# Retention's query times state in two parts, and a split last half of the attention's output

## The reference

```python
def step(r, qkv):                     # retention, chunk by chunk, per head
    s = einsum('bihd,bjhd->bhij', qf, kf) * intra
    o = einsum('bhij,bjhe->bihe', s, vf)
    o = o + einsum('bihd,bhde->bihe', qf, r) * q_dec
    r = r * c_dec + einsum('bjhd,bjhe->bhde', kf * k_dec, vf)
# then head_norm(o) * silu(g), a product with w_out, and a gate
# second layer: o = softmax(q k^T + decays) v, per head; x + gate * ((o * silu(g)) @ w_out)
```

## Time and profile before

| | us |
|---|---|
| median of 3 runs | 1717.95 (1715.57 to 1719.02) |
| the profiled execution's own time | 1717.91 |
| its span in the profile | 1716.1 |
| PE busy | 1661.4 (97%) |
| DVE busy | 812.5 (47%) |
| ACT busy | 611.4 (36%) |
| POOL busy | 380.7 (22%) |

### The profile page before, as it was taken

The page is one execution under the profiler, slowest core; times in us unless marked ns, Lnnn a source line. Parts: engine busy times, 40 slices in busy tenths (PEclk is TensorE's granted clock), DMA queues, the critical chain, the costliest instruction groups (busy, mean ns, idle before and its releaser), DMA issues.

```text
span 1716.1 us, 22075 instructions
## 1 busy us (share of the span) xinstructions
PE 1661.4 (97%) x8377; PEld 1326.9 (77%) x8377; DVE 812.5 (47%) x1661; ACT 611.4 (36%) x999; POOL 380.7 (22%) x501
## 2 busy tenths in 40 slices
PE   4999999999999999999999999999999998999998
PEld 3999998777876766667668888888788886788887
DVE  4654442212245445545543333665654015777774
ACT  4311121111134434434440223623322116566663
POOL 2111112111233333333322223414211100111000
PEclk8999999999999999999999999999999999999999
DMA  9544545563456767577663312232223625555531
GB/s 314 198 154 164 181 145 204 178 215 134 164 166 202 245 190 235 178 225 240 200 237 119 111 38 85 101 103 69 94 89 98 204 99 154 182 177 166 170 134 59
DMA packets 145338, 275.40 MB, mean 160 GB/s; under 512 B 18099, under 2 KB 64335, under 8 KB 145234
## 3 DMA queue, kind: packets, MB, share of 16 engines
q1 hardware_dynamic: 112450, 181.92, 33.2%
q0 software_dynamic: 32784, 92.08, 15.7%
HBM read 193.51 MB, written 80.43 MB: 160 GB/s over the span
## 4 chain that ended last, share of the span: by engine, by line
PE 84%; DVE 6%; ACT 4%; issue 3%; DMA 2%; POOL 1%; SPq 0%; DVEq 0%; POOLq 0%; ACTq 0%
PE trunk_ps L1150 29%; PE in_ps_o L541 12%; PE in_ps_o L537 11%; PE trunk_ps L1145 5%; PE tail_ps L2117 5%; PE tail_ps L2108 3%; PE trunk_ps L1193 3%; PE trunk_ps L1177 3%; PE tail_ps L2068 2%; PE tail_ps L2081 2%; PE in_ps_o L562 1%; PE trunk_ps L1188 1%; DVE room L1590 1%; POOL room L1460 1%; PE trunk_ps L1253 1%
## 5 line engine op out<-in xcount | busy, mean ns | idle before, releaser
L1150 PE MATMUL trunk_ps<-w_hi,hT_hi 128*128 128x512 f32 x880 | 360.0, 409 | 0.6 <-DVE w_lo L210 0.6
L1150 PE MATMUL trunk_ps<-w_hi,hT_lo 128*128 128x512 f32 x880 | 349.4, 397 | 0.0
L1150 PE MATMUL trunk_ps<-w_lo,hT_hi 128*128 128x512 f32 x880 | 347.0, 394 | 0.0
L1150 PEld LDWEIGHTS trunk_ps<-w_hi,hT_hi 128*128 128x128 f32 x880 | 165.5, 188 | 54.9 <-issue 17.6
L1150 PEld LDWEIGHTS trunk_ps<-w_lo,hT_hi 128*128 128x128 f32 x880 | 165.4, 188 | 43.0 <-issue 5.0
L1150 PEld LDWEIGHTS trunk_ps<-w_hi,hT_lo 128*128 128x128 f32 x880 | 165.2, 188 | 39.2
L210 DVE TENSOR_TENSOR w_lo<-w_raw,w_hi 128x1024 fp32r<-128x1024 f32 x76 | 96.5, 1271 | 115.3 <-ACT w_hi L198 110.0
L537 PE MATMUL in_ps_o<-hT_hi,w_hi 128*128 128x384 f32 x384 | 130.5, 340 | 0.4 <-DVE hT_lo L675 0.4
L537 PE MATMUL in_ps_o<-hT_hi,w_lo 128*128 128x384 f32 x384 | 129.1, 336 | 0.0
L537 PE MATMUL in_ps_o<-hT_lo,w_hi 128*128 128x384 f32 x384 | 129.1, 336 | 0.0
L541 PE MATMUL in_ps_o<-w_hi,hT_hi 128*128 128x512 f32 x288 | 114.4, 397 | 0.0
(11 more groups left out here) (274 smaller groups left out, 3291.8 us busy)
## 6 DMA issues: line engine op xcount, KB each, us to landing
w_raw<-in_a_w_in SPq DMA_DIRECT2D x96, 256.0 KB, 3.4
room<-in_state_ret SPq DMA_DIRECT2D x64, 256.0 KB, 4.0
out_state_sample<-room POOLq DMA_DIRECT2D x64, 256.0 KB, 6.7
room<-in_b_ada_w SPq DMA_DIRECT2D x24, 512.0 KB, 6.9
scratch_qkT<-room POOLq DMA_DIRECT2D x48, 192.0 KB, 2.2
scratch_v_hi<-room POOLq DMA_DIRECT2D x36, 256.0 KB, 2.6
scratch_v_lo<-room POOLq DMA_DIRECT2D x36, 256.0 KB, 3.1
scratch_o<-room POOLq DMA_DIRECT2D x36, 256.0 KB, 3.3
```

Source lines behind the costliest of these rows:

```text
L1150: ins = pe.matmul(ps[:, bank, :], h[:, k, t * P:(t + 1) * P], w[:, (C0 + j) % 2, k, :], start=k + m == 0, stop=k == KT - 1 and m == 2)
```

## The change

In the retention:

- the query chunk times state is done in six fp32r products (L1183 after the change) instead of two in float32 (L1193). For them ACT copies the new state (128x1024) and the next query chunk (128x256) into fp32r tiles (`hi_made`), and DVE subtracts (`query_low`, L1618, and `state_low`, L1623), for chunks 1 to 7 of each head;
- to make room, the values have one buffer in place of two: `load_v` of the next chunk waits for the output of this one (`o_done`), and stands in POOL's program ahead of this tile's gate product;
- queries and keys come chunk by chunk, 36 loads of 256 KB in pieces of 512 bytes, into three slots, where there were portions of three chunks; a slot is free once its chunk is scored and its query is split;
- `split_lo` moves from the end of an odd tile to the next even tile, behind `new_strips`, `query_low` and `state_low` and ahead of `statistics`; the fourth quarter so stands in tile 8;
- the rows that `half_turn` reads use other semaphores, with the same waits.

In the attention: in the last query tile, one output product each moves from units 4 and 6 to unit 7, where both stand behind the last turn of weights and ahead of the last values; the DVE's evacuation moves with them. The second half of the last tile is split in two quarters of 256 columns, in two banks, each with its own evacuation, addition and store.

```diff
-        v_hi, v_lo = (part(o, 2 * DV).rearrange("p (a b) -> p a b", a=2) for o in (0, 2 * DV))
-        k_hi, k_lo = part(4 * DV, DK), part(4 * DV + DK, DK)
-        s_hi, s_lo = part(4 * DV + 2 * DK, P), part(4 * DV + 2 * DK + P, P)
+        v_hi, v_lo = part(0, DV), part(DV, DV)
+        k_hi, k_lo = part(2 * DV, DK), part(2 * DV + DK, DK)
+        s_hi, s_lo = part(2 * DV + 2 * DK, P), part(2 * DV + 2 * DK + P, P)
+        state_hi, state_lo = pr.state_hi, pr.state_lo
+        q_hi, q_lo = pr.q_parts[:, 0], pr.q_parts[:, 1]
...
-        qk = [at(9216, 4, NB3), at(11776, 4, NB3)]
+        qk = [at(9216 + 4 * P * i, 4, P) for i in range(3)]
...
+        def qk_landed(h, c):
+            g = score_no(h, c)
+            return qk_in[g % 3], 16 * (g // 3 + 1)
 
...
+                h, c = g // T, order[g % T]
+                if g >= 3:
+                    ph, pc = (g - 3) // T, order[(g - 3) % T]
+                    sp.wait_ge(scored, g - 2)
+                    if pc == SELF:
                         sp.wait_ge(qs_ready, ph + 1)
+                    elif pc:
+                        sp.wait_ge(q_split, 7 * ph + pc)
                 for sem_, per_head in pr.qk_stored:
...
+                src = dr["qkT"][4 * h:4 * h + 4, :, c * P:(c + 1) * P].rearrange("a p t -> p a t")
+                sp.dma_start(qk[g % 3], src).then_inc(qk_in[g % 3], 16)
...
+                    if h + t == 0:
+                        load_qk(3)
+                    if T * h + t + 4 < T * RH:
+                        load_qk(T * h + t + 4)
...
-                    pe.wait_ge(state_new, n)
-                    q, _ = qk_of(h, c)
+                    pe.wait_ge(q_split, 7 * h + c)
+                    pe.wait_ge(state_split, 7 * h + c)
                     for a in range(2):
-                        ins = pe.matmul(ps[:, PS_O, :], q[:, a, :], state[:, a, :], start=False, stop=a == 1)
+                        for m, (q, r_) in enumerate(((q_hi, state_hi), (q_hi, state_lo), (q_lo, state_hi))):
+                            ins = pe.matmul(ps[:, PS_O, :], q[:, a, :], r_[:, a, :], start=False, stop=a == 1 and m == 2)
...
+                    if t + 1 < PT:
+                        act.wait_ge(state_new, PT * h + t + 1)
+                        act.copy(state_hi[:, :, :], state[:, :, :]).then_inc(hi_made, 1)
+                        act.wait_ge(*qk_landed(h, t + 1))
+                        act.copy(q_hi, qk_of(h, t + 1)[0]).then_inc(hi_made, 1)
...
-                if n >= 2:
-                    ph, pc = divmod(n - 2, PT)
+                if n:
+                    ph, pc = divmod(n - 1, PT)
                     pool.wait_ge(o_done, ph * T + pc + 1)
                 for dst, src in ((v_hi, "v_hi"), (v_lo, "v_lo")):
-                    pool.dma_start(dst[:, n % 2], dr[src][c * P:(c + 1) * P, h * DV:(h + 1) * DV].bitcast(F32R)).then_inc(v_in[n % 2], 16)
+                    pool.dma_start(dst, dr[src][c * P:(c + 1) * P, h * DV:(h + 1) * DV].bitcast(F32R)).then_inc(v_in, 16)
 
...
+                    if t < PT and PT * h + t + 1 < RH * PT:
+                        load_v(PT * h + t + 1)
...
+            def query_low(h, c):
+
+                dve.wait_ge(hi_made, 14 * h + 2 * c)
+                dve.tensor_tensor(q_lo, qk_of(h, c)[0], q_hi.bitcast(F32), ALU.subtract).then_inc(q_split, 1)
+
+            def state_low(h, c):
+
+                dve.wait_ge(hi_made, 14 * h + 2 * c + 1)
+                dve.tensor_tensor(state_lo[:, :, :], state[:, :, :], state_hi[:, :, :].bitcast(F32), ALU.subtract).then_inc(state_split, 1)
...
+                    if 0 < t < PT:
+                        query_low(h, t)
+                        state_low(h, t - 1)
                     if h == RH - 1:
                         half_low(t, 0)
+                    if t and t % 2 == 0:
+                        split_lo(pr, dve, C0 + h + 1, (C0 + h + 1) % 2, t // 2 - 1, gain=pr.gn_g[:, 0] if h + 1 == NG else None)
...
-                    if t % 2 and t < 2 * SUBS:
-                        split_lo(pr, dve, C0 + h + 1, (C0 + h + 1) % 2, t // 2, gain=pr.gn_g[:, 0] if h + 1 == NG else None)
...
-    COUNT = [[0, 2, 3, 3, 3, 2, 3, 0], [3, 2, 2, 1, 3, 2, 3, 0], [3, 1, 4, 0, 4, 0, 4, 0]]
+    COUNT = [[0, 2, 3, 3, 3, 2, 3, 0], [3, 2, 2, 1, 3, 2, 3, 0], [3, 1, 4, 0, 4, 0, 4, 0], [3, 1, 4, 0, 3, 0, 3, 2]]
+    HALF = CW // 2
...
+            def last_half(part, heads):
+
+                cols = slice(part * HALF, (part + 1) * HALF)
+                for h in heads:
+                    for m, (a, w) in enumerate(((oT_hi[:, h, :], pr.w_hi), (oT_hi[:, h, :], pr.w_lo), (oT_lo[:, h, :], pr.w_hi))):
+                        ins = pe.matmul(ps[:, part, 0:HALF], a, w[:, 1, h, cols], start=h + m == 0, stop=h == FH - 1 and m == 2)
+                if FH - 1 in heads:
+                    ins.then_inc(end_done, 1)
...
-                    count = COUNT[0 if s == 1 else 1 + order[s] // 4]
+                    count = COUNT[0 if s == 1 else 1 + (order[s] + 1) // 4 - int(order[s] == 3)]
...
-            for h in range(4):
-                end(STEPS - 1, 1, h, 0)
+            pe.wait_ge(o_split, 2 * (STEPS - 1) + 1)
+            for part in range(2):
+                last_half(part, range(4))
...
-                if s and i == 6:
+                if s and i == (7 if s + 1 == STEPS else 6):
...
+            last = 2 * (STEPS - 1)
+            for n, (c0, c1, bank) in enumerate(((0, CW, END), (CW, CW + HALF, 0), (CW + HALF, D, 1))):
+                width, into = c1 - c0, c0 % CW
+                dve.wait_ge(end_done, last + n + 1)
+                dve.wait_ge(added, last + n)
+                dve.tensor_tensor(tmp[:, into:into + width], ps[:, bank, 0:width], gate[:, c0:c1], ALU.mult).then_inc(end_out, 1)
+                if n < 2:
+                    dve.wait_ge(x1_in[n], 16 * STEPS)
+                dve.wait_ge(end_out, last + n + 1)
+                dve.tensor_tensor(x1[:, c0:c1], x1[:, c0:c1], tmp[:, into:into + width], ALU.add).then_inc(added, 1)
```

More of the change, by code:

```diff
@@ L823, in trunk @@
         ps_t = ps[:, 4:8, :].rearrange("p (a b) c -> p a b c", a=2)
-        qk_in = [sem(f"qk_in{i}") for i in range(2)]
-        v_in = [sem(f"v_in{i}") for i in range(2)]
+        qk_in = [sem(f"qk_in{i}") for i in range(3)]
+        v_in, hi_made, q_split, state_split = sem("v_in"), sem("hi_made"), sem("q_split"), sem("state_split")
         parted = sem("parted")
@@ L1050, in _ @@
                 sp.wait_ge(sem_, count)
-            load_qk(0)
+            for g in range(3):
+                load_qk(g)
             sp.dma_start(cols[:, :, :], pr.table["cols"].rearrange("p (a b) -> p a b", a=RH)).then_inc(cols_in, 16)
@@ L1058, in _ @@
             load_weights(1, 1)
-            load_qk(1)
             load_r(1)
@@ L1510, in _ @@
                     pool.dma_start(dr["o"][t * P:(t + 1) * P, h * DV:(h + 1) * DV], o_t).then_inc(o_stored[n % 2], 16)
-                    if t < PT and 8 * h + t + 2 < RH * PT:
-                        load_v(8 * h + t + 2)
             for n in range(M0, N):
@@ L2001, in _ @@
                 load_residual(STEPS - 1, c)
-            for c in range(2):
-                sp.wait_ge(added, 2 * STEPS - 1 + c)
-                sp.dma_start(rows_of(STEPS - 1, c)[0], x1[:, c * CW:(c + 1) * CW]).then_inc(y_last, 16)
-            sp.wait_ge(y_last, 32)
+            last = rows_of(STEPS - 1, 0)[0], *(rows_of(STEPS - 1, 1)[0][:, part * HALF:(part + 1) * HALF] for part in range(2))
+            for n, (c0, c1) in enumerate(((0, CW), (CW, CW + HALF), (CW + HALF, D))):
+                sp.wait_ge(added, 2 * STEPS - 1 + n)
+                sp.dma_start(last[n], x1[:, c0:c1]).then_inc(y_last, 16)
+            sp.wait_ge(y_last, 48)
         @block.tensor
@@ L2150, in _ @@
                 end(STEPS - 1, 0, h, END)
-            for h in range(4, FH):
-                end(STEPS - 1, 1, h, 0)
+            for part in range(2):
+                last_half(part, range(4, FH))
         @block.scalar
@@ L2407, in _ @@
             low_part(STEPS, 1)
-            for c in range(2):
-                end_out_of(STEPS - 1, c, 0 if c else END)
-                half = x1[:, c * CW:(c + 1) * CW]
-                dve.wait_ge(x1_in[c], 16 * STEPS)
-                dve.wait_ge(end_out, 2 * (STEPS - 1) + c + 1)
-                dve.tensor_tensor(half, half, tmp, ALU.add).then_inc(added, 1)
+            last = 2 * (STEPS - 1)
[8 more added lines that the diff above has]
+                dve.tensor_tensor(x1[:, c0:c1], x1[:, c0:c1], tmp[:, into:into + width], ALU.add).then_inc(added, 1)
 def build(nc, dram, table):
```

72 lines of the change are left out of this document (23 added, 49 removed).

## The result

The changed kernel takes **1733.37 us** (median of 4 runs, 1729.11 to 1735.37), the kernel before 1717.43 (4 runs); the ratio is 1.0088, with a 95% interval of 1.0076 to 1.0100. It is slower by some 15 us where 5 less were forecast, and outside the range. The profiled execution took 1732.21 us, its span is 1730.4.

What follows compares the result with a forecast made beforehand. PE, busy in 97% of the span, was taken as the bound; gains of 9.2, 7.0, 1.0 and 2.7 less costs of 5.8 and 8.8 made 5.3, so 1717.9 would become 1712.6 us, range 1703 to 1724.

Steps and rivals of the forecast that it cites:

- Query times state: Retention: six fp32r matmuls instead of two float32 ones save PE 0.33 us in each of 28 outputs, minus 9.2 us.
- Low weights behind the strips: Retention, tiles 4 and 6: PE's 0.88 us wait for the strips' banks goes, 8 times, minus 7.0 us.
- Tile 8: Retention: the fourth quarter of low weights comes late, PE waits 1.75 us in three heads, 0.5 in the last; plus 5.8.
- Values in one buffer: Retention, tiles 3, 5 and 7: values land late by 0.5 twice and 1.2 once in each head, plus 8.8 us.
- SP's queue: Retention, odd tiles: the query chunk's load stands behind a waiting weight load; no cost, as PE already waits for values.
- The last head's rows: Retention, tile 1 of the last head: the 1.8 us wait for half_turn's rows shrinks as PE comes later, minus 1.0.
- rival 3: Retention, tile 8: after each of four waits PE runs at the lower clock, 1.7 us each, 1719.4 us; chance 0.12.
- The attention's end: Attention's last query tile: moved products fill a gap and keep the clock up, 1.7 of the total; minus 2.7 us.
- Rival 2: Retention, odd tiles: values, query chunk and weights crowd; loads are the bound, 2 us late gives 1727.8 us; chance 0.18.

Runs made afterwards that it cites:

- split_alone: Kernel before with query times state in two parts in heads 0 to 2, two value pairs, chunk load ahead of weights, tile 1 reordered: 1717.35 us.
- one_pair: Kernel before with its values in one buffer, asked for when an output is done and ahead of the gate product: 1728.56 us, ratio 1.0057.
- qk_first: Changed kernel with the next query chunk's load ahead of the weight loads on SP's queue: 1725.36 us, ratio 1.0049.
- low_behind: Kernel before with the first three quarters of low weights behind the strips of tiles 2, 4 and 6: 1710.77 us, ratio 0.9957.
- tail_alone: Kernel before with only the change's part at the attention's end: 1715.81 us, ratio 0.9991.
- quarter_4: Changed kernel with the fourth quarter of low weights back at the end of tile 7: 1730.18 us, ratio 1.0076.

## Why the prediction was wrong

**Query times state, minus 9.2: right.** In tile 4 the first of the six starts at 639.10 and the next product at 640.46, 1.36 us against 1.72; 28 times 0.36 is 10.1. The low state is waited for once (0.5). From the start of the update to that of the product's second matmul it is 3.75 (636.94 to 640.69) against 4.10 in tile 5 before (641.85 to 645.95), 0.35 less. But split_alone shows that without the next term it is worth nothing; I had summed the two as independent.

**Low weights behind the strips, minus 7.0: right**, 7.2 by itself; in the changed kernel too no wait for the strips' banks is left before tile 8 of the last head.

**Tile 8, plus 5.8: right.** Three waits of 1.44 and one of 0.65, each 0.25 longer than listed, are 6.0:

```profile
581.25 0.50 PE L1141 MATMUL trunk_ps<-w_hi,hT_hi 128*128 128x512 f32 x1 [1.44 <-DVE w_lo L210]
```

**Values in one buffer, plus 8.8: right in size, partly by luck.** Eight waits of 7.2, 9.2 with the uncounted part, and some 10 in one_pair. But I had twelve, in tiles 3, 5 and 7 of every head; two of the eight stand in tile 1, none in the last head, and in three odd tiles the chunk's wait came first. By the Trainium skill ("DMA: Bandwidth & Descriptors", "Bandwidth") the loads would have landed later than my median. The time did come out slower, but not in that way: the value loads landed sooner than before (median 4.5 in heads 0 to 2, against 6.2), only they were asked for later.

**SP's queue, "I cost them at nothing of their own": this step failed.** The times that I gave the chunk were right: it goes out about when the values do (614.59 and 615.29) and is wanted just before them. What failed was the price of nothing. It is wanted 5.7 us after its issue and lands after 8.0; three waits came of it, 6.5 us, 7.3 with the uncounted part, where I had the values late by 0.5 in such a tile. The earlier trace rows were the right ones to read, and I set them aside; nor did I ask how long its slot had been free, which was 16 us. My reason, that PE waits for the values there anyway, held for most of these waits (in qk_first 5.0 of the 6.5 moved to the values), and still the chunk ahead of the weights won 8.0 us by the medians. The last head's rows, which I had at minus 1.0, are held up as well, and no longer in qk_first: the 1.8 at its start did go, but 0.9 and 3.5 came later, so plus 2.6.

**The clock, rival 3 at 0.12: a term that I had mostly in the wrong place.** I looked for it in tile 8. Three waits of 1.44 there left the clock at 1.00; behind the fourth place it was 0.54 (900 to 903), but so it was at that place in low_behind (0.66 from 874 to 879), which has the old fourth quarter. The large falls came behind waits for loads, for 7.5 us in all. By the page "TensorE: Matmul & The Clock Gate" of the Trainium skill, section "What's actually happening", the full clock is what activity earns and not the normal state; the falls agree, each right behind idle time, but the 2.20 us before 723.78 were idle time as well and left it at 1.00.

**The attention's end, minus 2.7: 1.7 of it had no ground.** I took it from a fall of the clock that other executions with the same end don't have. What is left of the term is 1.0, and tail_alone measured 1.5 (0.2 to 3.1). Between the two traces the end gives 2.3, because the kernel before happened to have that fall.

**Sum.** By stages, the changed kernel is 1.5 later at its first update (489.04 against 487.50), loses 15.4 from there to the product behind the last half turn (899.90 against 883.00), gains 0.3 up to the last value products (1712.89 against 1696.33) and 2.3 behind them: 14.3, as the spans have it. The terms of the retention are minus 10.1, minus 7.0, plus 6.0, 9.2, 7.3, 2.6, 0.7 for the low state and 7.5 for the clock, 16.2; the fall at 488 that only the kernel before had takes 1.7 off, so 0.9 of the 15.4 is open, and so is most of the 1.5 ahead of it. The four large terms that I had priced in the retention were off by less than 2 us each; the misses are a cost of nothing that was 7, the last head's rows, and the clock. Rival 2 comes nearest: values and chunk late by 16.5 us, 1.4 for each of its twelve tiles, which by its own sum is 1720.3; the rows and the clock, which it did not have, make up the rest. Its chance of 0.18 was too low because I judged each load by the landings of the kernel before, one by one, and did not add up what an odd tile now asks for at one time.

**What stays open.** Whether a given wait brings the clock down: one of 2.20 us in the third head did not, one of 1.97 in the last did. The 7.5 us are from one execution; how much of the clock's loss the change brings on average was not measured. And quarter_4 gave back some 3 of its 6 us in a way that I have only described by its waits.

## What to carry to other kernels

A load that is moved behind another on an in-order queue inherits every wait of that other: find when its buffer is free, when it goes out and which instruction takes it, before costing it at nothing. When a stage keeps the DMA engines fully busy, count what is asked for in the same microseconds and issue first what is wanted first; four steps put in another order turned 15 us lost into 5 won. And two terms can need each other: the shorter matmuls were worth 0 alone and about 7 us beside the moved low weights. Last, a stretch at the lower clock in one trace is no property of the kernel until a second trace has it too.

## What the runs showed of the hardware

- A wait of PE can cost nearly twice its length: after the 2.35 us before L1153 the granted clock was 0.51 for 3.3 us, which took 1.65 more. Its length did not decide: behind waits of 1.97, 1.98, 2.35 and 3.48 us the clock fell, and behind 1.83 in qk_first (0.55 from 766.8 to 770.0); behind 1.44 and 2.20 it stayed at 1.00, and behind 2.55 and 2.46 in quarter_4 (621.5 to 625.0 and 696.3 to 700.0).
- The same work falls to the lower level in one trace and not in another: the mean granted clock of the first 100 us, which the change does not touch, was 0.93 in the kernel before and 1.00 in the changed one, and the last value products of the old end took 4.61 us in one trace and 3.11 to 3.12 in three.
- Loads asked for by SP and by POOL land later when many are out: with four stores, two weight loads and a value pair out, the chunk for tile 4 landed in 8.0 us, at a DMA share of 1.01 and 1.09, where one of the same size issued at 598.38 took 2.9. The Trainium skill has a reason ("DMA: Bandwidth & Descriptors", "Issuing engines are not separate DMA queues"): what different engines start runs on the same 16 DMA engines and interleaves. With the values issued ahead of the stores the same bytes flowed (268 GB/s against 265), without the wait.
- The same subtraction L210 takes 1218 ns on average here and 1387 in the kernel before. Nothing of it was changed but its place. In the kernel before it takes 1.54 us in tile 4 of the second head, where it starts at 628.40 while POOL's product L1508 runs (627.58 to 628.85), and 1.22 in the changed kernel at 638.16, with no such product beside it. That POOL's product is the cause was not tested.
